# Two transformer blocks in one kernel: the expert gates spread over the partitions by DMA, the first expert behind the router, and a merged norm after the experts

## The chip, the cores and the metric

One Trainium2 chip, one core. The metric is the device time of one execution, in microseconds (us); the median of several executions counts. The engines are called PE (TensorE, matrix products), DVE (VectorE), ACT (ScalarE), POOL (GpSimd) and SP (SyncE). POOL and SP only start transfers here; each has a queue of its own, in which transfers start in the order written.

## The reference

All of it is float32, for 256 tokens of width 1024 and a context of 256 more:

```python
# block 1
h = h + concat(rmsnorm(fox(q_a, k_a, v_a)), rmsnorm(stick(q_b, k_b, v_b))) @ w_out   # from rmsnorm(x) @ w_in
h = h + cross_attention(rmsnorm(h), rmsnorm(mem)) @ w_xo
t = rmsnorm(h)                                  # (256, 1024)
g_val, g_idx = top_k(softmax(t @ w_rg + b_rg), 1)       # 4 groups
e_val, e_idx = top_k((t @ w_re + b_re)[group g_idx], 2) # 4 experts in each
gate = one_hot(experts) * (g_val * softmax(e_val))      # (256, 16)
for e in range(16):                             # hidden width 256
    h = h + gate[:, e:e+1] * ((silu(t @ w_gate[e]) * (t @ w_up[e])) @ w_down[e])
x = rmsnorm(h) * norm_final
# block 2, two layers
for l in range(2):
    sh1, sc1, ga1, sh2, sc2, ga2 = split(silu(c) @ w_mod[l] + b_mod[l])   # the same for ctx
    h = rmsnorm(x) * g1 * (1 + sc1) + sh1       # and hc from the context
    x = x + ga1 * (concat(fourier(h), mlstm(h, hc), mla(h, hc)) @ w_out[l])
    x = x + ga2 * (relu(mod(rmsnorm(x)) @ w_up[l])**2 @ w_down[l])
return rmsnorm(x) * g_final
```

## The kernel before, in words

**Layout.** Activations stand with their features on the 128 partitions: `res` holds 8 feature tiles of 512 columns, 256 of the context (`CTX`) and 256 of the tokens (`LAT`). Weights come from device memory as a stream of 350 pieces of 512 KB, a piece 128 x 1024 float32, into a ring of four (`ring`, SP's queue, L436). Precision is kept by splitting each operand into a high and a low part: ACT rounds a piece (`wh`, L532), DVE subtracts (`wl`, L1568), and PE makes three matmuls for each product, high x high, low x high and high x low (`prod`, L1019, recorded at L995). `split(n)` in the ACT and the DVE program takes the stream's pieces up to n, so its place in the program is the place of the conversion in the engine's order.

**Norms.** ACT squares two feature tiles at a time into slots of `sq` (L558), DVE adds them up in slot 3 (`add_square`, L1586), PE multiplies the sum by a matrix of ones in float32 (`norm`, L1041; the rows read `pair<-sq,table`), ACT makes the root with Ln and Exp (L568, L570), DVE scales (`uv`, L1608), ACT rounds (`uh`), DVE subtracts (`ul`, L1597 or, with a shift, L1599). Around it PE does matmuls whose result nobody reads (`turn_over`, "spins", L1039), in the numbers of the table `SPIN`.

**Modulation vectors.** silu(c) @ w_mod is not done on PE. DVE takes a tile of w_mod (512 KB, POOL's queue, L471) and forms two dot products with it, one for c and one for c_ctx (L1676, L1681). There are 48 such tiles for each layer. They are put by hand between other DVE work: for layer 0, 6 in the stick-breaking part, 4 in the output projection (`out1`), 4 in `xq`, 2 in `xo`, and 32 in the expert loop, two for each expert.

**Router and experts.** `few_rows` makes the 20 logits of each token as rows in a bank of PSUM, ACT copies them (L717), PE turns them to columns (L1276), DVE finds the groups, the experts and the weights in a chain of small operations (L1820 to L1847, results in `small`). Then PE spreads each of the 16 gate columns over all partitions: 64 matmuls of a broadcast column with the identity, ACT copying each pair to `gates` (L727). Eight matmuls with zeros open the four output banks. The experts run in halves of 128 hidden features: `gate_up(i, a, p)` (48 matmuls), then `down` of the half before (24 matmuls). The first expert stands unrolled ahead of the loop, the last behind it. After the last `down` comes norm `fin1`, then norm `n1_0` of the scaled result together with the context, then layer 0's projection.

**Layers.** The first three pieces of a layer's input projection share one loop over the norm's tiles (`together`, L1056). `gate_rows(d)` (DVE) and `log1p_rows` (ACT) prepare the mLSTM gates. After layer 1 comes norm `fin2`, and one transfer stores the result (L442).

Of the kernel before, what the change touches and what calls it, by code (L numbers as in the profile page):

```python
# [22 lines left out]
P = 128  # L23
D = 1024
# [59 lines left out]
NORM_LIST = [("mix", 4, 2), ("mem", 4, 2), ("fox", 2, 2), ("sb", 2, 2), ("xattn", 4, 2), ("ffn", 4, 2), ("fin1", 4, 2)]  # L84
for _l in range(NL):
    NORM_LIST += [(f"n1_{_l}", 8, 1), (f"cq_{_l}", 2, 1) if _l == 0 else (f"cq_{_l}", 1, 2), (f"ckv_{_l}", 1, 1)]
    NORM_LIST += [(f"n2_{_l}", 8, 1)]
# [4 lines left out]
for _i, (_name, _steps, _halves) in enumerate(NORM_LIST):  # L92
# [3 lines left out]
    _add += _steps if _name in LOOPED else _steps - 1  # L96
# [3 lines left out]
for _l in range(NL):  # L100
    U_STEPS += [(f"n1_{_l}", 8), (f"y_{_l}", 10), (f"n2_{_l}", 8)]
# [11 lines left out]
for _name, _n in U_STEPS:  # L113
# [4 lines left out]
SPIN = {"mix": (0, 19, 6), "sb": (5, 5, 6), "xattn": (6, 8, 6), "ffn": (6, 8, 6), "fin1": (24, 0, 4),  # L118
        "n1_0": (34, 17, 5), "n2_0": (7, 17, 5), "n1_1": (18, 17, 6), "n2_1": (5, 8, 5)}
# [3 lines left out]
OUT_NORMS = [_name for _name, _, _ in NORM_LIST if _name not in V_N and _name != "fin1"]  # L123
# [36 lines left out]
MOD_OUT, MOD_XQ, MOD_XO = 4, 4, 2  # L160
MOD_MOE = len(MOD_SB) + MOD_OUT + MOD_XQ + MOD_XO
assert MOD_MOE + N_UNIT == N_MOD
# [58 lines left out]
def build(nc, w_stream, mod_stream, c_rows, ml_dram, table_in, small_in, x_in, mem_in, ctx_in, out):  # L221
    with ExitStack() as stack:
# [92 lines left out]
        hroot = small[:, 140:144]  # L315
        prob = [sq[:, i, :] for i in range(2)]
# [23 lines left out]
        m_ge = tab("m_ge").rearrange("p (k t) -> p k t", k=2)  # L340

# [81 lines left out]
        def _(sp):  # L423
# [17 lines left out]
            sp.wait_ge(S("norm_out"), normed("fin2")[1])  # L441
            sp.dma_start(out, res[:, :, LAT]).then_inc(S("stored"), 16)  # L442
            sp.wait_ge(S("stored"), 16)

        @block.gpsimd
        def _(pool):
# [9 lines left out]

            def mod_loads(l):
# [7 lines left out]
                for g in range(l * N_MOD, (l + 1) * N_MOD):  # L465
                    if g >= l * N_MOD + 2:
                        pool.wait_ge(S("mod_used"), g - 1)
# [55 lines left out]
        def _(act):  # L523
# [36 lines left out]
            def root(name, p, n, width):  # L560
# [3 lines left out]
                if i:  # L564

                    sem, count = normed(NORM_LIST[i - 1][0])
                    act.wait_ge(S(sem), count)
                ch.link(act.activation(rstd[0:p, 0:n], norm_bank(name)[0:p, 0:n], ACT.Ln, bias=tab("eps")[0:p],  # L568
                                       scale=1.0 / width))
# [1862 lines left out]
```

## Time and profile before

| | |
|---|---|
| three runs | 1703.35, 1700.3, 1702.18 us; median 1702.18 |
| the profiled execution | 1705.07 us |
| its span, first to last instruction | 1703.2 us |
| mean granted TensorE clock | 0.98 of full speed |
| PE busy | 1619.8 us (95%) |
| PE weight loads (beside PE) | 1396.6 us (82%) |
| DVE, ACT, POOL busy | 1077.3, 771.8, 96.6 us (63, 45, 6%) |
| read from device memory | 248.84 MB, 147 GB/s over the span |
| chain that ended last, by engine | PE 81%, DVE 12%, ACT 3%, issue 3%, DMA 1% |

Busy times are sums over stages with different limits. The stages, by the profile's time: attention parts up to 252, `out1` to 257, cross-attention with its projections to 336, router 340 to 361, experts 361 to 634, layer 0 from 657, the end at 1703. The profiled execution took 2.9 us more than the median.

### The profile page before, as it was taken

How to read it: one execution, taken by the hardware profiler on the slowest of the kernel's cores; microseconds unless marked ns; L12 is line 12 of the kernel's file. 1: busy time of each engine (PE TensorE's matmuls, PEld its weight loads, DVE VectorE, ACT ScalarE, POOL GpSimd, SP SyncE). 2: the span in 40 equal slices, each digit the busy share in tenths (PEclk: the TensorE clock that was granted, in tenths of full speed). 3: DMA queues.
4: the chain of work that ended last, by engine and by line, in shares of the span. 5: the costliest groups of instructions: out<-in, count | busy, mean ns of one | idle time of the engine just before them, and what ended most of it. 6: DMA issues, size and time to landing. Idle time of an engine off the chain costs nothing.

```text
span 1703.2 us, 27364 instructions
## 1 busy us (share of the span) xinstructions
PE 1619.8 (95%) x9992; PEld 1396.6 (82%) x9992; DVE 1077.3 (63%) x1800; ACT 771.8 (45%) x1306; POOL 96.6 (6%) x160
## 2 busy tenths in 40 slices
PE   7999988999999999999889999999999898899997
PEld 7988567899999996775668788888887785799997
DVE  5544677658888887932584755555556944765554
ACT  5544444444444445343462642134323354665562
POOL 0000100000000000000020000000000000100000
PEclk9999999999999999999999999999999999999998
DMA  7633435337777770332114355455542351155552
GB/s 286 203 121 106 119 121 197 126 106 245 244 246 246 244 236 25 99 123 63 34 29 136 136 189 177 142 165 189 166 145 91 112 158 30 45 166 186 173 184 86
DMA packets 70841, 250.96 MB, mean 147 GB/s; under 512 B 7760, under 2 KB 10976, under 8 KB 70640
## 3 DMA queue, kind: packets, MB, share of 16 engines
q1 hardware_dynamic: 54000, 189.43, 33.9%
q0 software_dynamic: 16768, 60.54, 12.5%
q8 instruction: 49, 0.80, 0.2%
q14 instruction: 24, 0.20, 0.0%
HBM read 248.84 MB, written 1.09 MB: 147 GB/s over the span
## 4 chain that ended last, share of the span: by engine, by line
PE 81%; DVE 12%; ACT 3%; issue 3%; DMA 1%; DVEq 0%; SPq 0%; ACTq 0%
PE pair L995 79%; DVE uv L1608 1%; DVE sq L2086 1%; DVE wl L1568 1%; ACT wh L532 1%; DVE sq L1586 1%; DVE small L1635 1%; DVE sq L1644 1%; PE pair L1162 1%; PE pair L1039 1%; DVE uh_f L1681 1%; ACT sq L558 0%; ACT sq L600 0%; DVE ul L1597 0%; DVE spent L1676 0%
## 5 line engine op out<-in xcount | busy, mean ns | idle before, releaser
L995 PE MATMUL pair<-uh,wh 128*128 128x256 f32 (+3 forms) x1840 | 579.0, 315 | 13.1 <-DVE ul L1597 4.5
L1568 DVE TENSOR_TENSOR wl<-ring,wh 128x1024 fp32r<-128x1024 f32 x350 | 426.9, 1224 | 245.0 <-ACT wh L532 237.9
L995 PE MATMUL pair<-uh,wl 128*128 128x256 f32 (+3 forms) x1840 | 574.3, 312 | 0.0
L995 PE MATMUL pair<-ul,wh 128*128 128x256 f32 (+3 forms) x1840 | 572.7, 311 | 0.0
L532 ACT ACTIVATE wh<-ring 128x1024 fp32r<-128x1024 f32 x350 | 367.5, 1052 | 267.9 <-PE pair L995 262.3
L995 PEld LDWEIGHTS pair<-uh,wh 128*128 128x128 f32 (+1 forms) x1840 | 343.5, 187 | 42.6 <-issue 13.8
L995 PEld LDWEIGHTS pair<-uh,wl 128*128 128x128 f32 (+1 forms) x1840 | 343.6, 187 | 25.6
L995 PEld LDWEIGHTS pair<-ul,wh 128*128 128x128 f32 (+1 forms) x1840 | 343.3, 187 | 24.9
L995 PE MATMUL pair<-hh,wh 128*128 128x512 f32 (+1 forms) x512 | 172.7, 337 | 0.8
L995 PE MATMUL pair<-hh,wl 128*128 128x512 f32 (+1 forms) x512 | 172.0, 336 | 0.0
L995 PE MATMUL pair<-hl,wh 128*128 128x512 f32 (+1 forms) x512 | 172.0, 336 | 0.0
L995 PEld LDWEIGHTS pair<-hh,wh 128*128 128x128 f32 x512 | 97.1, 190 | 12.0 <-issue 2.0
L995 PEld LDWEIGHTS pair<-hl,wh 128*128 128x128 f32 x512 | 97.2, 190 | 10.0
L995 PEld LDWEIGHTS pair<-hh,wl 128*128 128x128 f32 x512 | 97.1, 190 | 10.0
L2207 DVE TENSOR_TENSOR hl<-sq,hh 128x512 f32 (+1 forms) x64 | 35.8, 559 | 95.9 <-ACT hh L954 95.8
L949 ACT ACTIVATE sq<-pair 128x512 f32<-128x512 f32 (+1 forms) x64 | 31.3, 489 | 107.4 <-PE pair L995 107.4
L995 PE MATMUL pair<-hidh,wl 128*128 128x256 f32 x256 | 72.6, 284 | 0.0
L995 PE MATMUL pair<-hidh,wh 128*128 128x256 f32 x256 | 72.5, 283 | 0.0
L995 PE MATMUL pair<-hidl,wh 128*128 128x256 f32 x256 | 72.4, 283 | 0.0
L1039 PE MATMUL pair<-spin 128*128 128x512 f32 x250 | 65.9, 414 | 0.0
L995 PE MATMUL pair<-wh,uh 128*128 128x256 f32 (+1 forms) x192 | 57.2, 298 | 3.0 <-ACT qkp L793 3.0
L471 POOL DMA_DIRECT2D uh_f<-in_mods x48 | 36.0, 751 | 418.1 <-DVE macc L1681 267.4
(259 smaller groups left out, 2080.7 us busy)
## 6 DMA issues: line engine op xcount, KB each, us to landing
ring<-in_w_stream SPq DMA_DIRECT2D x350, 512.0 KB, 3.9
uh_f<-in_mods POOLq DMA_DIRECT2D x48, 512.0 KB, 6.1
mod_w<-in_mods POOLq DMA_DIRECT2D x48, 512.0 KB, 3.8
ml<-ml_dram POOLq DMA_DIRECT2D x4, 512.0 KB, 8.1
table<-in_table SPq DMA_DIRECT2D x1, 1849.5 KB, 12.0
res<-in_x SPq DMA_DIRECT2D x4, 256.0 KB, 3.9
res<-in_mem SPq DMA_DIRECT2D x1, 1024.0 KB, 14.3
res<-in_ctx POOLq DMA_DIRECT2D x1, 1024.0 KB, 6.1
```

The lines of the kernel that those rows point to most:

```text
L471: pool.dma_start(mod_w[l][g % 2], src).then_inc(S(f"mod_in{g % 2}"), 16)
L532: act.activation(wh[:, s, :], ring[:, s, :], ACT.Copy).then_inc(S("w_hi"), 1)
L949: act.activation(r, bank[(b0 + j) % 4][:, 0:n], ACT.Relu).then_inc(S("job_emptied_act"), 1)
L995: ins = pe.matmul(*operands, **flags)
L1039: pe.matmul(bank[b], spin[:, 0:P], spin[:, :], start=True, stop=True)
L1162: last = pe.transpose(bank[6][:, to * P:(to + 1) * P], prob[i % 2][:, j * P:(j + 1) * P], ident)
L1568: tt(wl[:, s, :], ring[:, s, :], wh[:, s, :].bitcast(F32), ALU.subtract).then_inc(S("w_lo"), 1)
L1586: tt(sq[0:p, 3, 0:n], sq[0:p, 3, 0:n], sq[0:p, t % 2, 0:n], ALU.add).then_inc(S("norm_add"), 1)
L1608: last = stt(o, src, g, r, ALU.mult, ALU.mult)
L1635: dve.tensor_reduce(smv(i, 0, 0, g), b, AX_X, ALU.max, negate=True).then_inc(S("sm_max"), 1)
L1644: last = ts(p, p, smv(i, 1, k), None, ALU.mult)
L2207: tt(hl[:, d, 0:n].rearrange("p a b -> p (a b)"), sq[:, 2 + j % 2, 0:n], hh[:, d, 0:n].rearrange("p a b -> p (a b)").bitcast(F32), ALU.sub ...
```

## The change

1. **Norms.** In every norm that isn't in a loop DVE no longer adds the last square. PE sums slot 3, and the slot of the last square with a second pair of ones-matmuls.
2. **Modulation tiles.** In `out1` the fourth tile stands behind the adds and the split instead of ahead of them. The cross-attention takes a tile (at `i == 1`), `xo` three instead of two. The experts have 30 instead of 32, none in the first and none in the last half expert.
3. **Router.** The logits go to a bank of the experts' output (`rt_bank`). PE goes on behind them with the first half expert's gate and up, with the turning of the logits between two of its steps. The context's squares are summed here (norm `ctx`). Of the 20 spins 4 are left.
4. **Gates.** PE turns the 16 gate columns to rows (2 transposes), ACT copies them, and POOL writes them to device memory (`gate_dram`, 16 KB) and reads them back to all partitions in three transfers, of 2, 6 and 8 gates. DVE waits for the first ahead of the first half expert's multiplication, for the other two ahead of the loop.
5. **End of the experts.** `fin1` and `n1_0` become one norm for the tokens: squares are taken with a weight and the epsilon is changed to fit. The context's half of layer 0's first three pieces is done apart, with its own tiles, and around the norm. 75 spins are gone. `fin1`'s own norm and its scaling of `res` go into layer 0's projections.
6. **Layers.** `gate_rows` at j = 11 and 13 instead of 2 and 3; the gate biases and `log1p_rows` move to j = 0 to 3.
7. **Store.** Four transfers of 256 KB, each when its two tiles are scaled, instead of one of 1 MB.

The core of the diff:

```diff
-SPIN = {"mix": (0, 19, 6), "sb": (5, 5, 6), "xattn": (6, 8, 6), "ffn": (6, 8, 6), "fin1": (24, 0, 4),
-        "n1_0": (34, 17, 5), "n2_0": (7, 17, 5), "n1_1": (18, 17, 6), "n2_1": (5, 8, 5)}
+SPIN = {"mix": (0, 19, 6), "sb": (5, 5, 6), "xattn": (6, 8, 6), "ffn": (6, 8, 6),
+        "n2_0": (7, 17, 5), "n1_1": (18, 17, 6), "n2_1": (5, 8, 5)}
...
-MOD_OUT, MOD_XQ, MOD_XO = 4, 4, 2
+MOD_OUT, MOD_XQ, MOD_XAT, MOD_XO = 4, 4, 1, 3
...
-            sp.wait_ge(S("norm_out"), normed("fin2")[1])
-            sp.dma_start(out, res[:, :, LAT]).then_inc(S("stored"), 16)
+            for t in range(4):
+                sp.wait_ge(S("fin2_tile"), 2 * t + 2)
+                sp.dma_start(out[:, 2 * t:2 * t + 2, :], res[:, 2 * t:2 * t + 2, LAT]).then_inc(S("stored"), 16)
...
+            def gate_loads():
+
+                pool.wait_ge(S("gate_rows"), 1)
+                pool.dma_start(gate_dram, logit_rows[0:NE, :]).then_inc(S("gate_out"), 16)
+                pool.wait_ge(S("gate_out"), 16)
+                for k, e in enumerate((slice(0, 2), slice(2, 8), slice(8, NE))):
+                    pool.dma_start(gates[:, e, :], gate_dram[e, :].rearrange("(o e) t -> o e t", o=1)
+                                   .to_broadcast([P, e.stop - e.start, T])).then_inc(S(f"gate_in{k}"), 16)
...
-            for e in range(NE // 2):
-                act.wait_ge(S("gate_full"), e + 1)
-                act.activation(gates[:, 2 * e:2 * e + 2, :], bank[4 + e % 2][:, :].rearrange("p (a t) -> p a t", a=2),
-                               ACT.Copy).then_inc(S("gate_in"), 1)
-            split(S_MOE + 2)
+            root("ctx", P, T, D, rstd[:, T:2 * T])
+            split(S_MOE + 3)
+            act.wait_ge(S("gate_full"), 1)
+            act.activation(logit_rows[0:NE, :], rt_bank[0:NE, 0:T], ACT.Copy).then_inc(S("gate_rows"), 1)
+            split(S_MOE + 4)
...
+                slots = [3] if name in LOOPED or steps == 1 else [3, (steps - 1) % 2]
+                for slot in slots:
+                    if slot != 3:
+
+                        pe.wait_ge(S("norm_sq"), SQ_AT[name] + steps)
+                    for j in range(HALVES[name]):
+                        last = mm(norm_bank(name)[0:p, 0:n], ones[0:p, 0:p], sq[0:p, slot, j * n:(j + 1) * n],
+                                  start=(slot == 3 and j == 0), stop=(slot == slots[-1] and j == HALVES[name] - 1))
...
+            gate_up(0, 0, S_MOE, first=True)
+            norm("ctx", P, T)
+            turn_over(4, 5)
+            pe.wait_ge(S("rt_gate"), 1)
+            for b in range(TB):
+                last = pe.transpose(rt_bank[0:NE, b * P:(b + 1) * P], rt[:, b, 44:60], ident)
+            last.then_inc(S("gate_full"), 1)
...
+            dve.wait_ge(S("gate_in0"), 16)
             moe_unit(0, -1)
+            for k in (1, 2):
+                dve.wait_ge(S(f"gate_in{k}"), 16)
             with dve.Fori(0, MOE_TURNS) as i:
...
+                    for j in range(3):
+                        outs[j] = (outs[j][0](),) + outs[j][1:]
+                        for k in range(3):
+                            half("c1_0", CTX, j, k)
+                    for k in range(3, KT):
+                        if k == 5:
+                            norm("n1_0", P, T)
+                        for j in range(3):
+                            half("c1_0", CTX, j, k)
+                    for k in range(KT):
+                        for j in range(3):
...
+                            last = half("n1_0", LAT, j, k)
```

The order of the instructions, at the two places where most is moved. PE from the router's logits to the expert loop; `L995` and `L1049` are the matmul helper before and after, `rt_gate` is DVE's signal that the weights are ready. Before:

```order
L1276 MATMUL pair<-table,logit_rows 128x20 [waits rt_rows]
L1276 MATMUL pair<-table,logit_rows 128x20
L1039 MATMUL pair<-spin 128x512 x20
L995 MATMUL pair<-table,small 128x128 [waits rt_gate]
L995 MATMUL pair<-table,small 128x128 x7
L995 MATMUL pair<-table,small 128x128 [waits gate_in]
L995 MATMUL pair<-table,small 128x128 x3
```

The last two rows come six times. After, behind the four steps of the first half expert that stand ahead of the logits, the 36 matmuls of its other steps run between the second row and the third:

```order
L1342 MATMUL pair<-table,logit_rows 128x20 [waits rt_rows]
L1342 MATMUL pair<-table,logit_rows 128x20
L1049 MATMUL pair<-sq,table 128x256 [waits norm_add]
L1049 MATMUL pair<-sq,table 128x256
L1049 MATMUL pair<-sq,table 128x256 [waits norm_sq]
L1049 MATMUL pair<-sq,table 128x256
L1093 MATMUL pair<-spin 128x512 x4
L1362 MATMUL pair<-table,small 16x128 [waits rt_gate]
L1362 MATMUL pair<-table,small 16x128
L1049 MATMUL pair<-uh,hidl 128x256 [waits gate_rows,moe_lo]
L1049 MATMUL pair<-uh,hidl 128x256 x7
L1383 UNCONDITIONAL_BRANCH [waits norm_rstd]
```

So the 64 broadcasts with their waits for ACT's copies have left PE. DVE's rows at the start of the experts, after; the branch is the entry of the loop, and behind it stands the subtraction for the sixth piece of the experts' stream:

```order
L1663 TENSOR_TENSOR wl<-ring,wh 128x1024 [waits w_hi] x2
L1972 TENSOR_TENSOR eg<-eg,gates 128x256 [waits moe_silu,gate_in0]
L1978 TENSOR_TENSOR eg<-pair,eg 128x256 [waits moe_eg,moe_up]
L1982 TENSOR_TENSOR hidl<-eg,hidh 128x256 [waits moe_hi]
L2010 UNCONDITIONAL_BRANCH [waits gate_in2,gate_in1]
L2010 ISA
L1663 TENSOR_TENSOR wl<-ring,wh 128x1024 [waits w_hi]
```

Before, the first of these multiplications waited for ACT's eight copies, and nothing stood between the first half expert and the loop. DVE at the end of the experts, from the last piece's subtraction on, before:

```order
L1568 TENSOR_TENSOR wl<-ring,wh 128x1024 [waits w_hi]
L1676 ISA spent,macc<-uh_f_105,uv 128x1024 [waits mod_used,mod_in1]
L1676 ISA macc 128x1
L1681 ISA uh_f_105,macc<-uh_f_105,uv 128x4x256
L1681 ISA macc 128x1
L1893 COPY modv<-macc 128x8 [waits mod_used]
L1914 TENSOR_TENSOR res<-pair,res 128x2x256 [waits moe_down,macc_out]
```

And after:

```order
L1663 TENSOR_TENSOR wl<-ring,wh 128x1024 [waits w_hi] x2
L2025 SCALAR_TENSOR_TENSOR uv<-res,gmod,rstd 128x256 [waits norm_rstd,macc_out]
L2025 SCALAR_TENSOR_TENSOR uv<-res,gmod,rstd 128x256
L1695 SCALAR_TENSOR_TENSOR ul<-uv,modv,uh 128x256 [waits u_h]
L2025 SCALAR_TENSOR_TENSOR uv<-res,gmod,rstd 128x256
L1695 SCALAR_TENSOR_TENSOR ul<-uv,modv,uh 128x256 [waits u_h] x2
L2044 TENSOR_TENSOR res<-pair,res 128x2x256 [waits moe_down] x4
L2025 SCALAR_TENSOR_TENSOR uv<-res,gmod,rstd 128x256 x2
L1695 SCALAR_TENSOR_TENSOR ul<-uv,modv,uh 128x256 [waits u_h] x2
L1682 TENSOR_TENSOR sq<-sq 128x512 [waits norm_sq]
```

The modulation tile has left this place, and the context's first three tiles stand ahead of the residual's adds.

## Rows read from the trace of the kernel before

**Rows 1.** Windows: us, busy of PE, PEld, DVE, ACT, POOL, clock, DMA, GB/s

```profile
346.00:361.00 15.00, 13.54 (x95) 12.18 (x95) 5.14 (x35) 6.19 (x15) 0.00 (x0) 0.99 0.12 36
400.00:600.00 200.00, 200.00 (x1688) 200.00 (x1687) 166.56 (x241) 87.69 (x117) 18.03 (x24) 1.00 0.75 244
634.00:658.00 24.00, 20.17 (x87) 15.52 (x86) 19.07 (x41) 12.23 (x23) 0.00 (x0) 1.00 0.12 38
```

**Rows 2.** The same, spins (L1039) alone: PE, PEld, clock, DMA, GB/s

```profile
634.00:658.00 24.00, 18.18 (x75) 14.02 (x75) 1.00 0.12 38
```

**Rows 3.** PE's waits: us in total, times, longest

```profile
PE pair L995 <- DVE sq L1586: 17.0, 8, 8.1
```

**Rows 4.** Timeline of PE, ones-matmuls: start, us, instruction

```profile
8.12 2.05 PE L995 MATMUL pair<-sq,table 128*128 128x256 f32 x4 [8.12 <-DVE sq L1586]
...
336.42 1.13 PE L995 MATMUL pair<-sq,table 128*128 128x256 f32 x4 [0.80 <-DVE sq L1586]
...
337.20 2.20 PE L1039 MATMUL pair<-spin 128*128 128x512 f32 x8
```

**Rows 5.** The page's costliest groups, DVE's lo parts; timeline of a modulation tile

```profile
L1568 DVE TENSOR_TENSOR wl<-ring,wh 128x1024 fp32r<-128x1024 f32 x350 | 426.9, 1224 | 245.0 <-ACT wh L532 237.9
...
257.94 1.22 DVE L1676 CUSTOM_DVE_ANT_1 spent<-uh_f,uv 128x1024 f32<-128x1024 f32 x1
```

**Rows 6.** Timeline and window at the norm before the cross-attention

```profile
261.77 2.08 PE L995 MATMUL pair<-sq,table 128*128 128x256 f32 x4 [3.07 <-DVE sq L1586]
...
264.84 1.27 DVE L1608 SCALAR_TENSOR_TENSOR uv<-res,table,rstd 128x256 f32<-128x256 f32 x3 [1.99 <-ACT rstd L570]
...
262.00:264.00 2.00, 2.00 (x5) 1.61 (x6) 0.85 (x1) 0.12 (x1) 0.00 (x0) 0.50 0.79 252
```

**Rows 7.** Timeline of DVE and PE around the router

```profile
338.55 1.28 DVE L1608 SCALAR_TENSOR_TENSOR uv<-res,table,rstd 128x256 f32<-128x256 f32 x3 [0.71 <-ACT rstd L570]
...
347.05 0.20 DVE L1820 COPY small<-pair 128x40 f32<-128x40 f32 x1 [0.92 <-PE pair L1276]
...
352.69 7.58 PE L995 MATMUL pair<-table,small 128*128 128x128 f32 x64 [0.91 <-DVE small L1847]
...
375.26 0.28 PE L995 MATMUL pair<-uh,wh 128*128 128x256 f32 x1
```

**Rows 8.** DMA issues: transfer, queue, count, KB each, median us to landing

```profile
ml<-ml_dram POOLq DMA_DIRECT2D x4, 512.0 KB, 8.1
...
ml<-ml_dram POOLq DMA_DIRECT2D x4, 256.0 KB, 7.5
out_dram<-res SPq DMA_DIRECT2D x1, 1024.0 KB, 4.8
...
lw<-ml_dram POOLq DMA_DIRECT2D x2, 256.0 KB, 5.1
...
ml_dram<-rows_buf POOLq DMA_DIRECT2D x4, 8.0 KB, 1.8
```

**Rows 9.** Windows beside ring and modulation loads, and beside broadcasts (columns as rows 1)

```profile
290.00:292.00 2.00, 1.31 (x7) 1.07 (x7) 1.94 (x3) 0.60 (x1) 0.28 (x1) 1.00 1.00 358
...
846.00:848.00 2.00, 1.35 (x11) 0.95 (x9) 0.42 (x2) 0.03 (x1) 0.00 (x0) 1.00 1.00 264
...
850.00:852.00 2.00, 1.44 (x12) 1.25 (x12) 2.00 (x5) 2.00 (x5) 0.00 (x0) 1.00 0.65 145
```

**Rows 10.** Timeline from the last expert to layer 0's first copy

```profile
634.34 5.63 PE L1039 MATMUL pair<-spin 128*128 128x512 f32 x24
...
657.70 0.47 PE L995 MATMUL pair<-uh,wh 128*128 128x512 f32 x1 [0.95 <-DVE ul L1599]
...
674.56 0.58 ACT L793 ACTIVATE qkp<-pair 96x512 f32<-96x512 f32 x1
```

**Rows 11.** Timeline of PE in layer 1's first pieces

```profile
1324.60 0.45 PE L995 MATMUL pair<-uh,wh 128*96 128x512 f32 x1 [1.53 <-DVE wl L1568]
...
1343.32 0.47 PE L995 MATMUL pair<-uh,wh 128*128 128x512 f32 x1 [1.71 <-DVE wl L1568]
```

More of the change, by code:

```diff
@@ L81 @@
 N_LCOLS = 1408
-NORM_LIST = [("mix", 4, 2), ("mem", 4, 2), ("fox", 2, 2), ("sb", 2, 2), ("xattn", 4, 2), ("ffn", 4, 2), ("fin1", 4, 2)]
+NORM_LIST = [("mix", 4, 2), ("mem", 4, 2), ("fox", 2, 2), ("sb", 2, 2), ("xattn", 4, 2), ("ffn", 4, 2), ("ctx", 4, 2),
+             ("n1_0", 4, 2), ("fin1", 4, 2)]
 for _l in range(NL):
-    NORM_LIST += [(f"n1_{_l}", 8, 1), (f"cq_{_l}", 2, 1) if _l == 0 else (f"cq_{_l}", 1, 2), (f"ckv_{_l}", 1, 1)]
+    if _l:
+        NORM_LIST += [(f"n1_{_l}", 8, 1)]
+    NORM_LIST += [(f"cq_{_l}", 2, 1) if _l == 0 else (f"cq_{_l}", 1, 2), (f"ckv_{_l}", 1, 1)]
     NORM_LIST += [(f"n2_{_l}", 8, 1)]
@@ L715, in _ @@
             split(S_RT + AHEAD)
+            act.wait_ge(S("ctx_in"), 16)
+            for t in range(4):
+                square("ctx", t, res[:, 2 * t:2 * t + 2, CTX], P, 512)
             act.wait_ge(S("rt_logits"), 1)
-            act.activation(logit_rows[0:20, :], bank[6][0:20, 0:T], ACT.Identity,
+            act.activation(logit_rows[0:20, :], rt_bank[0:20, 0:T], ACT.Identity,
                            bias=tab("b_route", 20)).then_inc(S("rt_rows"), 1)
@@ L783, in _ @@
                     split(p0 + j + AHEAD)
-                    if j in (1, 2):
-                        log1p_rows(rows[j - 1][:, 1, :], rows[j - 1][:, 2, :], "ml_f", 2 * l + j, "ml_ln")
+                    if l == 0 and j == 1:
+                        for t in range(4):
+                            square("fin1", t, res[:, 2 * t:2 * t + 2, LAT], P, 512)
+                    if l == 0 and j == 5:
+                        root("fin1", P, T, D, sq[:, 2, 0:T])
+                    if j in (2, 3):
+                        log1p_rows(rows[j - 2][:, 1, :], rows[j - 2][:, 2, :], "ml_f", 2 * l + j - 1, "ml_ln")
                     b = full(act, f"mqk_{l}", j)
@@ L1327, in _ @@
             down(MOE_TURNS, UNIT_TURN - 1, S_MOE + N_TURN - 1, final=True)
-            norm("fin1", P, T)
             for l in range(NL):
@@ L1350, in _ @@
                 for j in range(2, 8):
+                    if l == 0 and j == 4:
+                        norm("fin1", P, T)
                     tiles_of(f"mqk_{l}", j, p0 + j, MD if j < 7 else P, cols if j < 4 else ALL)
```

281 lines of the change are left out of this document (177 added, 104 removed).

## The prediction

> **What bounds the kernel now.** I read the page's totals first: TensorE (PE) is busy for 1619.8 of 1703.2 us (in the table above). The windows then say where a change can pay. In the expert loop PE has no gap: 1688 matmuls in 200 us, 0.118 us each, with DVE at 166.56 [rows 1], so there only fewer PE instructions would help. The other two windows of that group lie at its ends. From 346 to 361 PE is busy for 13.54 of 15 us, but with gate broadcasts; from 634 to 658 it is busy for 20.17 of 24, and 18.18 of that is spins [rows 1, 2]. Next I read the waits: PE waits 17.0 us in 8 places for the last add of squares [rows 3]. Last the timelines of each place, for the chain that ends there.
>
> **The added ones-matmuls.** A norm's last pair of ones-matmuls no longer waits for one DVE add, and a second pair is added. An add takes 0.69. A pair takes 0.78 at full clock (336.42 to the spins at 337.20) and about 1.5 at the start of the program, where four rows take 2.05 [rows 4]. So at mix the extra pair costs 1.5 less the add: +0.9. At mem and fox PE runs through and the add was hidden, so the pair is paid whole: +0.85 at mem; at fox, where PE follows a stretch of small matmuls, I take the half clock, twice 0.78 less a little, +1.3. cq_0 gets a second matmul of 512 columns behind small ones too: +1.3 by the same reckoning. fin1's norm, moved into layer 0's projections where PE is full, is two pairs: +1.75. sb 0 and n2_1 -0.5 (a wait for the add). Sum **+5.6**; ends: 0, if the removed adds pay everywhere, and 8, if every pair is paid whole.
>
> **The moved modulation tiles.** One tile is two DVE operations of 1.22 us [rows 5]. At out1 the fourth tile stood ahead of the last adds, and PE stood still for 3.07 until 261.77 [rows 6]. Now the adds go first, but the tile is next and norm xattn's first scaling (264.84) comes behind it: 263.25 earliest, 0.5 gained at the end of it (-0.5), as root and ul follow. In the cross-attention the new tile stands ahead of the third row maximum (L1635); PE's next scores and everything behind it, up to the xo matmuls, move by 2.44 and a little: +2.7. Sum **+2.2**; ends 0 (a gap of the engines there takes it up) and 5.
>
> **The router and the first expert.** Frame: times of the profile, the shift above left out. xo's third tile, 2.44 us, stands between the split and the first scaling at 338.55. Without the last add DVE comes to it 0.9 earlier, so scaling starts at 340.1. The router's matmuls end at 347.5. PE goes on with gate and up of the first half expert, 48 matmuls (5.7), and the logits' transposes inside; DVE starts its chain of small operations at 349.85. That chain took from 347.05 until PE was released at 352.69, 5.6 [rows 7], so weights are ready at 355.45. PE has ended its 48 matmuls at 354.0, does norm ctx (two pairs, 1.6, and a root on ACT that starts behind it), 4 spins, and transposes at 357.0. ACT does root, one split (1.05) and the copy (0.5): gate_rows at 358.4. PE's 8 zeroing matmuls (1.1) and 48 more matmuls end at 365.1. The 64 broadcasts, 7.5 us [rows 7], are gone. What takes their place is a queue of four transfers on POOL. The write of 16 KB: 8 KB took 1.8 [rows 8], so 360.6 with its issue, and the first broadcast moves from 361.9. The first broadcast, 256 KB: 5.1 as lw<-ml_dram, so 365.7, and down(0,0) starts at 367.6 after two multiplications, a rounding and a subtraction (0.4 each), ending at 370.5. The other two are 1.75 MB. This is the **unknown price**. DVE waits for both before the loop, and behind that wait stands the lo split of the sixth piece, which PE's third gate-and-up needs. Rows for broadcasts out of device memory are slow: 512 KB took 8.1 to land [rows 8], and the windows beside them move 264 and 145 GB/s, with ring pieces in it [rows 9]. Rows of the other end: 358 GB/s at 290 to 292, with wholly different rows of memory for each partition. I take 190 GB/s (between 145 and 264, and these are the same kind of transfer): 2.1 MB take 11.0 from 361.9, and two ring pieces between them 2 more: 375. A lo part of 1.22 behind it [rows 5]: PE starts at 376.3 against 375.26 [rows 7], +1.0, and 1.7 more, because after some 5 us with nothing to do the clock falls: behind the gap of 3.07 the window shows 0.50 [rows 6]. **+2.7**; ends -4.7 and +17.4 (rivals A and D).
>
> Here a page stands against my price. The Trainium skill ("DMA: Bandwidth & Descriptors", "Anatomy of one DMA — SWDGE (gpsimd) path") puts such a transfer at about 2.0 us plus bytes over 436 GB/s; the estimate by it for 2 MB is 6.8 us, and my sum would come out near 17 below the profile instead of 10. The trace does not agree for broadcasts of this kernel: 8.1 us for 512 KB.
>
> **The end of the experts.** Before, the last down ends at 634.34 and DVE ends its modulation tile and adds to the residual, PE sums squares, DVE scales, squares again, and layer 0's first matmul starts at 657.70; its three pieces (72 matmuls of 512 columns) end at 674.5, where the first copy starts [rows 10]. After: one norm for both, and the context half of the same matmuls needs nothing of it. DVE makes context tiles from 634.1 (the modulation tile that ran until 636.4 is gone), adds at 636.9 to 639.3, and PE does 36 of the context half's matmuls meanwhile. The last squares are in at 643.5, the two pairs end at 645.4, root at 646.75, and with a scaling, a rounding and an ul the LAT half starts at 648.6: 72 matmuls of 256 columns, 8.5 us, end at 657.0. With the short pauses between context tiles I put 2.3 on it for a lower clock: 659.3. **-15.1**; ends -18 (no clock loss) and -9 (rival C). The total of PE work left is 2 x 8.5 + 1.9 = 18.9 us behind 634.4, so nothing below 653.3 is possible.
>
> **Layers and tail.** gate_rows at j = 11 and 13 leaves the place where, in layer 1, PE waits 1.53 and 1.71 for a lo split [rows 11]: **-3.2** (ends -3.2 and 0, if the convolutions or the later place wait for the same). In layer 0 the same rows plus fin1's eight scalings stand at j = 10 to 13; DVE has spare time there, nothing. The store of 1 MB landed in 4.8 [rows 8]; now four of 256 KB, three of them under the scaling. The last: between 1.8 (8 KB) and 4.8, by bytes 2.6, and 2.9 behind its three neighbours: **-1.9**.
>
> **Sum.** 5.6 + 2.2 + 2.7 - 15.1 - 3.2 - 1.9 = -9.7 against 1705.07, the profiled execution's time, so 1695.4. The median of the three runs lies 2.9 below that execution: **1692.5 us**.
>
> **Rivals.** A, the loads are fast (0.2): at 358 GB/s all three land at 367.7, down(0,0) ends at 370.6 and the third gate-and-up follows at once: -4.7 in place of +2.7, no clock loss, sum -17.1, median **1685.1**. For it: every other load of this size; against it: the broadcast rows. B, they are slower than I take (0.12): four broadcasts of 256 KB, issued within 1.5 us, land 7.5 after issue each [rows 8], 1.05 MB in 9 us or 118 GB/s; the third gate-and-up is 6.7 later, sum -3.0, **1699.2**. C, the clock (0.12): 75 spins are taken out between 634 and 658 and the matmuls that replace them come with pauses for context tiles. Behind the 3.07 us gap of [rows 6], the window has PE at 0.50 though spins ran on. Should the half clock hold for the stage, 72 matmuls of 256 columns take twice 8.5, of which some 6 stay on the path: sum -3.7, **1698.5**. The Trainium skill ("TensorE: Matmul & The Clock Gate", Part 1) has the throttled state as the default that activity releases, which speaks against taking spins out; the trace agrees in that gap. D, slower (0.06): the loads stand behind mod loads and ring pieces, with all partitions reading one 16 KB, at about 80 GB/s. gate_in2 lands at 390, the third gate-and-up waits until 391, PE idle for 20 us: 15.7 and the clock's 1.7, +17.4 in place of +2.7, sum +5.0, **1707.2**. It decides from a landing after 385 on (the sum is zero there). That the change does not do what it says I can leave out: the order of the engines shows every move.
>
> **How the numbers follow.** The forecast has 0.5, A 0.2, B 0.12, C 0.12, D 0.06. A difference of 0.2% (3.4 us) is about what a measurement of this kernel can tell from none. Of B and C, at -3.0 and -3.7, half lies within it; so same 0.12, slower 0.06, faster 0.82. The range is 1685 to 1700: it takes in A's value, B and C, and the bounds of the small terms (+2.4 and -5.6 at the ones-matmuls, 3.2 at the layers); outside lie D, the sum of several bad ends and A with a good clock.
>
> **What would show it.** In the changed kernel's profile: gates<-gate_dram in the list of DMA issues with its time to landing (mine: some 5, 9 and 13 us); PE's wait for wl ahead of the third gate-and-up, 5.8 us; the LAT half's first matmul some 14 us behind the last down, with the clock of the window of 24 us behind it at 0.8 or more; no wait for wl in layer 1's first pieces; PE waits for adds of squares down from 17.0. It would be wrong if the loads land within 7 us of their issue or beyond 25, or if the clock in that window is 0.5.

## The result, and the profile after

| | before | after |
|---|---|---|
| median | 1702.1 us (4 runs) | 1676.88 us (4 runs, 1672.28 to 1681.26) |
| ratio | | 0.9861, 95% interval 0.9836 to 0.9885 |
| span of the profiled execution | 1703.2 us | 1673.3 us |
| mean granted TensorE clock in it | 0.980 | 0.984 |

Two later series of the same changed kernel gave ratios of 0.9888 (0.9858 to 0.9918) and 0.9877 (0.9857 to 0.9898). All 17 of its runs together have the median 1679.3; 49 runs of the kernel before in three later series have 1699.7, and they reach from 1691.6 to 1706.7. So the change is worth about 20 us, not the 30 that the two first profiles differ by, and not the 9.7 that I forecast. The predicted range ended at 1685 and the median lies below it.

Each execution also has its mean granted clock on record, and that explains most of the spread. Over the 49 runs of the kernel before it goes from 0.978 (1706.7 us) to 0.989 (1693.4); a straight line through them gives 1.39 us for each 0.001, and leaves a scatter of 1.6 us of 3.5. Measured from that line, that is against the kernel before at the same granted clock, the changed kernel is 22.2, 22.6 and 23.3 us faster in its three series. The line is an estimate from these runs, used again below.

The page after, its totals and the part of its waits that answers to [rows 3] (before, PE waited 17.0 us in 8 places for the last add):

```profile
PE 1596.2 (95%) x9959; PEld 1383.8 (83%) x9959; DVE 1069.2 (64%) x1790; ACT 768.2 (46%) x1308; POOL 98.6 (6%) x164
```

```profile
PE pair L1049 <- DVE sq L1682: 7.9, 2, 7.7
```

The waits for adds are gone but for the program's start (7.7). Part of them only moved: PE now waits 8.2 us in 5 places for the low parts of L1693, where it waited 4.5 in 4 for those of L1597. A wait of 4.5 us is new: the first `down` waits for the first gates (PE's first row below). The router in the timelines of POOL, DVE and PE, which answers to [rows 7]:

```profile
351.59 0.53 POOL L469 DMA_DIRECT2D gate_dram<-logit_rows  x1 [16.96 <-ACT logit_rows L755]
353.56 1.63 POOL L472 DMA_DIRECT2D gates<-gate_dram  x3 [1.45 <-DMA gate_dram<-logit_rows]
```

```profile
360.79 0.43 DVE L1972 TENSOR_TENSOR eg<-eg,gates 128x256 f32<-128x256 f32 x1 [7.29 <-DMA gates<-gate_dram]
...
365.86 1.23 DVE L1663 TENSOR_TENSOR wl<-ring,wh 128x1024 fp32r<-128x1024 f32 x1 [3.21 <-DMA gates<-gate_dram]
```

```profile
362.78 0.58 PE L1049 MATMUL pair<-hidh,wh 128*128 128x256 f32 x1 [4.50 <-DVE hidl L1982]
...
368.06 0.29 PE L1049 MATMUL pair<-uh,wh 128*128 128x256 f32 x1
```

The three broadcasts land 7.2, 9.0 and 10.9 us after their own issues, where I had some 5, 9 and 13. The last is issued at 354.7 and lands at 365.6, 12.0 us after the first issue; my sum had 14.4 (375 less 360.6). The loads didn't creep. Windows of 2 us over them (the columns are those of rows 1) show 323 and 415 GB/s, with PE all but idle:

```profile
354.00:356.00 2.00, 2.00 (x20) 2.00 (x19) 0.00 (x0) 0.00 (x0) 1.19 (x3) 1.00 0.82 287
356.00:358.00 2.00, 2.00 (x20) 2.00 (x18) 0.00 (x0) 0.00 (x0) 0.00 (x0) 1.00 0.64 188
358.00:360.00 2.00, 0.28 (x3) 0.07 (x1) 0.00 (x0) 0.00 (x0) 0.00 (x0) 1.00 0.99 323
360.00:362.00 2.00, 0.00 (x0) 0.00 (x0) 0.85 (x2) 0.22 (x1) 0.00 (x0) 0.81 0.99 415
362.00:364.00 2.00, 1.22 (x5) 1.23 (x6) 0.42 (x1) 2.00 (x4) 0.00 (x0) 0.50 0.70 295
```

The last two windows also show the half clock (0.50, that is 1.2 of 2.4 GHz) behind the wait of 4.5 us; `down` ran at it. The end of the experts, PE and then ACT, which answers to [rows 10]:

```profile
628.57 0.36 PE L1049 MATMUL pair<-uh,wh 128*128 128x256 f32 x1 [1.27 <-DVE ul L1695]
...
636.37 0.92 PE L1049 MATMUL pair<-sq,table 128*128 128x256 f32 x3
```

```profile
650.25 0.58 ACT L847 ACTIVATE qkp<-pair 96x512 f32<-96x512 f32 x1
```

From the last `down`'s end (627.30) to layer 0's first copy it is 22.95 us where it was 40.06. The merged norm's ones-matmuls run 9 us behind the last `down`, with the context's matmuls on both sides of them. The tokens' half starts at 641.28, 14.0 behind the last `down` as forecast, and the window of 24 us behind it has a granted clock of 0.93.

Because single executions wander, I read the stages from all profiles of this study: four of the kernel before and its variants, ten of the changed kernel and its variants, each only where the stage is untouched. The figures are lengths between the same two PE instructions, in us; the difference is that of the means.

| stage | before | after | difference | forecast |
|---|---|---|---|---|
| first norm to norm mem | 32.0, 32.3, 33.8 | 35.5 in seven of ten; 33.7, 35.2, 36.5 | +2.7 | +0.9 (mix; the pair alone 1.5) |
| norm mem to the forgetting attention's scores | 58.9, 61.3, 61.3 | 59.2 in eight of ten; 61.1, 63.1 | -0.8 | +0.85 (mem) |
| the attention parts, to the spins of norm sb | 123.6, 124.8 | 117.7 to 123.5, eight profiles | -3.8 | +1.3 (fox) |
| end of out1 to xq | 8.5, 9.5, 9.9 | 7.7 | -1.6 | -0.5 |
| xq to the scores | 23.5 to 23.7 | 25.0 to 25.1 in six of seven; 23.5 | +1.2 | 0 |
| scores to xo | 20.2 to 21.1 | 21.1 to 23.2 | +1.6 | +2.7 |
| end of xo to the third gate-and-up | 40.2 to 41.2 | 38.7 to 40.5, four profiles | -1.2 | +2.7 |
| last down to layer 0's first copy | 40.1 to 40.2 | 22.9 to 23.0 | -17.1 | -15.1 |
| from there to layer 1's norm | 624.8 to 626.6 | 624.2 to 630.0 | +2.1 | +3.05 |
| that norm to n2_1 | 202.4, 202.8 | 197.0 to 198.5 | -5.0 | -3.7 |
| n2_1 to fin2 | 190.9 | 188.4 to 191.4 | -1.0 | 0 |
| fin2 to the end | 10.1 | 7.9 to 8.0 | -2.2 | -1.9 |

The first row starts behind the wait for the add, so it holds the price of the extra pair alone. In the first profiles that is 1.7 (3.19 us for the ones-matmuls instead of 1.49), near the 1.5 of the forecast; what the removed add gives back lies ahead of the row.

### The profile page after: what moved, and what is told of

Its sections match the earlier page's. It is cut to its first block, busy times and chain, and to the rows that moved or that the text cites. A ratio compares the mean times of both kernels' runs of the same rounds, so it can differ in the third digit from the quotient of the medians.

```text
span 1673.3 us, 27283 instructions
## 1 busy us (share of the span) xinstructions
PE 1596.2 (95%) x9959; PEld 1383.8 (83%) x9959; DVE 1069.2 (64%) x1790; ACT 768.2 (46%) x1308; POOL 98.6 (6%) x164
## 4 chain that ended last, share of the span: by engine, by line
PE 83%; DVE 9%; ACT 3%; issue 3%; DMA 1%; DVEq 0%; SPq 0%; ACTq 0%
PE pair L1049 81%; ACT wh L552 1%; DVE uv L1704 1%; DVE sq L2228 1%; PE pair L1223 1%; DVE sq L1740 1%; DVE wl L1663 1%; DVE small L1731 1%; PE pair L1093 1%; DVE ul L1693 0%; DMA gates<-gate_dram 0%; DMA uh_f<-in_mods 0%; DVE uh_f L1777 0%; ACT sq L621 0%; DVE spent L1772 0%
## 5 line engine op out<-in xcount | busy, mean ns | idle before, releaser
L1049 PE MATMUL pair<-uh,wh 128*128 128x256 f32 (+3 forms) x1864 | 583.5, 313 | 14.0 <-DVE ul L1693 8.2
L1049 PE MATMUL pair<-uh,wl 128*128 128x256 f32 (+3 forms) x1864 | 577.9, 310 | 0.0
L1049 PE MATMUL pair<-ul,wh 128*128 128x256 f32 (+3 forms) x1864 | 576.4, 309 | 0.0
L1049 PEld LDWEIGHTS pair<-uh,wh 128*128 128x128 f32 (+1 forms) x1864 | 347.9, 187 | 42.1 <-issue 14.3
L1049 PEld LDWEIGHTS pair<-uh,wl 128*128 128x128 f32 (+1 forms) x1864 | 347.8, 187 | 24.0
L1049 PEld LDWEIGHTS pair<-ul,wh 128*128 128x128 f32 (+1 forms) x1864 | 347.5, 186 | 23.4
L1049 PE MATMUL pair<-hh,wh 128*128 128x512 f32 (+1 forms) x512 | 172.7, 337 | 0.8
L1049 PE MATMUL pair<-hh,wl 128*128 128x512 f32 (+1 forms) x512 | 172.0, 336 | 0.0
L1049 PE MATMUL pair<-hl,wh 128*128 128x512 f32 (+1 forms) x512 | 172.0, 336 | 0.0
L1049 PEld LDWEIGHTS pair<-hh,wh 128*128 128x128 f32 x512 | 97.1, 190 | 11.9 <-issue 2.0
L1049 PEld LDWEIGHTS pair<-hh,wl 128*128 128x128 f32 x512 | 97.1, 190 | 10.1
L1049 PEld LDWEIGHTS pair<-hl,wh 128*128 128x128 f32 x512 | 97.2, 190 | 10.0
L1049 PE MATMUL pair<-hidh,wh 128*128 128x256 f32 x256 | 73.7, 288 | 4.5 <-DVE hidl L1982 4.5
L1049 PE MATMUL pair<-hidh,wl 128*128 128x256 f32 x256 | 73.6, 288 | 0.0
L1049 PE MATMUL pair<-hidl,wh 128*128 128x256 f32 x256 | 73.5, 287 | 0.0
L1049 PE MATMUL pair<-wh,uh 128*128 128x256 f32 (+1 forms) x192 | 57.2, 298 | 3.0 <-ACT qkp L847 3.0
L1777 DVE CUSTOM_DVE_ANT_0 mod_w<-mod_w,mod_c 128x1024 f32<-128x1024 f32 x48 | 58.5, 1219 | 0.0
L1777 DVE CUSTOM_DVE_ANT_1 uh_f<-uh_f,uv 128x1024 f32<-128x1024 f32 x48 | 58.5, 1218 | 0.0
```

Source lines behind the costliest of these rows:

```text
L1049: ins = pe.matmul(*operands, **flags)
L1777: return dve.tensor_tensor_reduce(out=mod_w[l][k], in0=mod_w[l][k], in1=mod_c[l][which], scale=1.0, scalar=0.0, op0=ALU.mult, op1=ALU.add, ...
```

## The experiments

**The changed kernel again, twice.** No edit.

> The changed kernel once more, unchanged, as the base of the three below on the same chip. Theory 'structure': the stretches in which TensorE is granted half its clock follow from PE's own gaps, so they fall at the same places as in the first profile (258 to 262, 288 to 292, 336 to 341, 360 to 368, 630 to 634, 756 to 766, 798 to 804, 1374 to 1380) and none at 92 to 100; time 1674 to 1680. Rival 'luck': they move from execution to execution, and one of about 3 us at 92 to 100, as the kernel before had, may come back; time 1672 to 1684.

> The changed kernel, unchanged, as the base of a_sb_fill on the same chip, and for a third profile: 1676 to 1681. The part behind the experts (last down to the first copy of layer 0) should take 22.9 to 23.0 us again; the loop of layer 1's MLP takes 2.72 or 2.83 for a tile (both were seen with this kernel).

Medians 1681.07 (6 runs) and 1679.31 (7), spans 1679.3 and 1670.2. The third profile has most of its half-clock stretches where the first had them, but not those at 630 to 634 (0.61 in the first) and 798 to 804 (0.51 in the first, 0.93 in the third). The second lacks the one behind the last `down` too. It has one that the first lacks, behind PE's wait of 2.13 us for the last stick-breaking head, a wait that stands in all three:

```profile
214.00:228.00 14.00, 11.74 (x24) 6.17 (x25) 3.44 (x7) 2.41 (x4) 0.00 (x0) 0.55 0.10 35
```

The first profile has 1.00 in the same window. The attention part takes 122.35 in the second profile against 118.06 and 118.08 in the others. Both theories hold in part: places belong to the program, but not each comes in each execution. The experts' end took 22.93 and 22.98, as expected.

**Fox's add put back in the changed kernel.**

```diff
-    _add += _steps if _name in LOOPED else max(_steps - 2, 0)
+    _add += _steps if _name in LOOPED else _steps - 1 if _name in ADDED else max(_steps - 2, 0)   # ADDED = ("fox",)
```

> The changed kernel with one thing undone: norm fox gets its DVE add of the last square back, and one pair of ones-matmuls. Theory 'blocked queue': before, that add stood in DVE's order ahead of a modulation tile and of the stick-breaking operations and waited there for ACT's squares; PE's wait of 1.92 us at that place and the half clock behind it came from it. Then this run is 4 to 7 us slower than the changed kernel, with a PE wait for sbt of about 2 us behind the norm. Rival 'price of a pair', by which I forecast +1.3 for the removal: this run is 1 to 1.5 us faster than the changed kernel.

Median 1680.19 (5 runs) against 1681.07: no difference that these runs can tell. PE's wait came back as expected, and the half clock behind it (194 to 201):

```profile
194.21 1.19 PE L1050 MATMUL pair<-qk 64*128 64x256 f32 x2 [1.92 <-DVE sbt L1837]
```

The changed kernel waits 0.51 here (the row at 192.41 of its first profile). But this execution lacked the stretch at 214 to 228, and its attention part took 121.8. So the 4 to 7 us slower that I expected didn't come; whether it is the rival's 1 to 1.5 us faster, five and six runs can't tell.

**Fox alone, in the kernel before.**

```diff
+                if name == "fox":
+                    return
```
(in DVE's `add_square`; PE waits for the square and sums slots 3 and 1)

> The kernel before with norm fox alone changed: no DVE add of its last square, a second pair of ones-matmuls. Forecast's term: +1.3 (about 1702 against 1700.7). Theory 'blocked queue': PE's wait of 1.92 for sbt doesn't come, and the part from the first stick-breaking scores to its end takes 118 to 123 us instead of 123.6 to 124.8; runs 2 to 4 below before.

Ratio 0.9998 (0.9983 to 1.0013), 12 runs. PE's wait is 0.51 and not 1.92, so the queue was blocked as the theory says, but the gain of 2 to 4 us isn't there. Its profile had half-clock stretches at 94 to 100 and 216 to 226, and took 121.7 for the part. The add's removal is worth less than 3 us, and it isn't a loss of more than 2.2; my +1.3 lies inside these bounds.

**All norms, in the kernel before.** The diff of the change for `add_square`, `norm` and the count of the adds, nothing else. It also gives an extra pair to `fin1` and `n1_0`, which are still two norms in this kernel.

> The kernel before with the norms' part of the change alone (no last add, a second pair of ones-matmuls, in every norm that isn't in a loop). The forecast's own term was +5.6 less the +1.75 of the moved norm, so about 1706 (+3.5). Theory 'blocked queue': the fox part turns by some -6 to -7, out1's add saves about 1 more, so 1696 to 1700 (-2 to -6).

Ratio 0.9991 (0.9969 to 1.0013): -1.6 us, between -5.3 and +2.2. My +3.9 for this part (5.6 less 1.75; the +3.5 above is a slip) is outside, and so is the far end of the rival's range. The trace has what the extra pairs cost and save: +1.7 at mix (35.5 us to norm mem), and 8.6 us from out1's end to xq, against 8.5, 9.5 and 9.9. The granted clocks say more. Their mean is 0.987 over these 12 runs, where the kernel before has 0.984, and against the line of the kernel before at the same clock they are 3.6 us slower (+-0.8 by their own scatter). By this estimate the pairs cost about what I forecast, and the full clock, which was granted for longer, gave it back. Which of the removed waits raised the clock wasn't tried; at fox alone (the run above) it stayed at 0.984.

**Gates by matmuls in the changed kernel.**

```diff
-            for b in range(TB):
-                last = pe.transpose(rt_bank[0:NE, b * P:(b + 1) * P], rt[:, b, 44:60], ident)
+            for e in range(NE // 2):     # 4 broadcast matmuls each, into two banks
+                last = mm(gate_banks[e % 2][...], small[:, w:w + 1].to_broadcast([P, P]), ident, start=True, stop=True)
...
-                    if g == MOD_MOE + 2:
-                        gate_loads()
```

> The changed kernel, but the gates are spread by 64 matmuls and 8 copies on ACT, behind the first half expert's gate and up, instead of by the DMA. No transfer, no wait of 4.5 us for the first gates, no half clock behind it. Theory 'the DMA is a loss here': PE pays 7.5 us and the first down follows at once, so the third gate-and-up comes 1 to 3 us earlier than with the DMA: 1 to 3 us faster than the changed kernel. Rival 'the DMA pays': the matmuls cost their 7.5 us and the waits that they replace were 1.2 and 4.5 with 2 of half clock, so the same within 0.5, or slower by up to 3 if ACT's copies hold the broadcasts back.

Median 1677.64 (4 runs) against 1681.07 (6), within their noise. From the logits' transposes to the third gate-and-up 24.27 us, against 25.30, 24.57 and 23.42 in the three profiles with the DMA. So the way of the gates makes no difference that can be seen: the 7.5 us of matmuls and the transfers' latency cost the same. `down` ran at half clock, wholly or in part, in all eight profiles with the DMA, and at full clock in the two with matmuls, which had no wait there. That the stage is shorter than before must then come from what both kernels have, the first gate-and-up in the time of DVE's chain; that was not undone by itself.

**The broadcasts twice.**

```diff
+                pool.wait_ge(S("gate_in1"), 16)
+                pool.wait_ge(S("gate_in2"), 16)
+                for k, e in ((1, slice(2, 8)), (2, slice(8, NE))):   # the same two transfers again
```

> The changed kernel, but the second and third broadcast are made twice, the second time when both have landed, and DVE waits for the second time: 1.75 MB more on the disputed path. Theory 'the broadcast moves like any other load' (320 to 415 GB/s in the first profile): the third gate-and-up comes some 6 to 8 us later, latency of the second pair with it. Rival 'slow broadcasts', my 190 GB/s: 10 to 12 us later. The rate can be read from windows of 2 us without the other engines' noise.

POOL issues the second pair at 372.54 and DVE goes on at 379.90, 7.4 us for 1.84 MB with the latency. The windows:

```profile
374.00:376.00 2.00, 0.06 (x1) 0.00 (x0) 0.00 (x0) 0.00 (x0) 0.00 (x0) 1.00 0.93 310
376.00:378.00 2.00, 0.00 (x0) 0.00 (x0) 0.00 (x0) 0.00 (x0) 0.00 (x0) 0.56 1.00 411
378.00:380.00 2.00, 0.00 (x0) 0.00 (x0) 0.10 (x1) 0.00 (x0) 0.00 (x0) 0.50 0.38 160
```

The logits-to-third-gate-and-up stretch is 31.15 us against 23.4 to 25.3: 6 to 8 more, as the theory of an ordinary load said. A broadcast out of device memory, with rows of 6 and 8 KB for a partition, moves 411 GB/s. My 190 is refuted as the rate at which these transfers move. By the rule of the Trainium skill ("DMA: Bandwidth & Descriptors", "Anatomy of one DMA — SWDGE (gpsimd) path"), 1.84 MB would take an estimated 6.2 us; the trace's 7.4, for two transfers and POOL's issue, is 1.2 above it.

**The broadcasts in a chain of 1, 7 and 8 gates.**

```diff
-                for k, e in enumerate((slice(0, 2), slice(2, 8), slice(8, NE))):
+                for k, e in enumerate((slice(0, 1), slice(1, 8), slice(8, NE))):
+                    if k == 1:
+                        pool.wait_ge(S("gate_in0"), 16)
```

> The changed kernel with the three broadcasts cut as 1, 7 and 8 gates, and the second and third issued only when the first has landed. Theory 'shared queue': the first broadcast of 256 KB took 7.2 us from issue because the other two ran beside it; alone, 128 KB land in 3 to 4.5, so the wait of 4.5 us ahead of the first down shrinks to 1 to 2, and the other two, at the 320 to 415 GB/s of the first profile, land at most 1 us later than they did (12.3 us behind the first issue). Rival 'latency': a broadcast out of device memory takes 6 to 7 us whatever its size; then the first wait stays at 4 and the others land 6 us later, 5 us slower.

One execution, 1679.12 us. 128 KB landed in 4.6 us where 256 KB took 7.2, and the first wait shrank from 4.50 to 1.94. The wait for the others grew:

```profile
361.40 0.38 PE L1051 MATMUL pair<-hidh,wh 128*128 128x256 f32 x1 [1.94 <-DVE hidl L1984]
...
368.23 0.38 PE L1051 MATMUL pair<-uh,wh 128*128 128x256 f32 x1 [2.20 <-DVE wl L1665]
```

Logits to third gate-and-up 24.45 us, no gain: what had been one wait is two. The experts behind it took 260.9 us where the changed kernel takes 259.2, a loss of 1.6. The rival, 6 to 7 us whatever the size, is refuted. The theory of the shared queue fits the first landing, though the run changed size and company together: at 411 GB/s half the size is an estimated 0.3 us of the 2.6. It gives nothing, since the loop waits for all gates.

**Spins in three waits.**

```diff
-SPIN = {"mix": (0, 19, 6), "sb": (5, 5, 6), "xattn": (6, 8, 6), "ffn": (6, 8, 6),
+SPIN = {"mix": (0, 19, 6), "sb": (5, 5, 6), "xattn": (6, 16, 6), "ffn": (6, 16, 6),
...
                     pe.wait_ge(S("w_lo"), p0 + 2)
+                    turn_over(6, 7)
```

> The changed kernel with spins in three waits of PE: 8 more behind the norms xattn and ffn (waits of 2.36 and 2.35), 6 behind the last down (wait of 1.27). Theory 'gap, then half clock': the half-clock stretches at 258 to 262, 336 to 341 and 630 to 634 go, each worth 1 to 1.5 us; the trace gains 3 to 4 by layer 0 and the runs' median about 3. Rival 'the clock falls for another reason' (a fixed spacing in time, or the float32 matmuls): the stretches stay or move, no gain, and the spins themselves cost up to 1.

The three stretches are gone; the first two:

```profile
258.00:262.00 4.00, 4.00 (x19) 3.33 (x18) 3.83 (x6) 1.04 (x3) 0.02 (x1) 1.00 0.43 128
336.00:341.00 5.00, 4.30 (x21) 2.97 (x19) 5.00 (x15) 2.26 (x6) 0.75 (x1) 1.00 0.60 202
```

In the changed kernel's first profile these windows have 0.60 and 0.66, and 630 to 634 has 0.61:

```profile
258.00:262.00 4.00, 4.00 (x25) 4.00 (x24) 3.58 (x11) 2.65 (x6) 0.00 (x0) 0.60 0.31 114
```

(This execution ran 4 to 6 us behind, and none of its windows at 262 to 290, 341 to 362 and 634 to 700 has the half clock either.) For two of the three places all profiles together bear the gap theory out. Behind the waits of 2.3 us at xattn and ffn the half clock came in six of seven profiles each, and with the spins in none of three each. For the third place this run shows nothing: behind the last `down` four of the seven profiles without spins have full clock too. The theory is wrong about the price in two of three. xq to the scores went from 25.0 to 23.2 (and took 23.5 in the one profile that had the wait and kept full clock). But the rows of the router took 7.52 as before, and the experts' end 22.94 as before, since DVE's tiles set the pace there: in all ten profiles it takes 22.93 to 22.98, in three at half clock and in seven at full. Median 1676.24 (5 runs), ratio 0.9874 (0.9852 to 0.9896): no gain that the runs can tell.

**The same, and spins for the last stick-breaking head.**

```diff
+                    if h == NF:
+                        turn_over(8, JOBS.number("xkv", 6) % 4)
```

> a_fill3 with 8 spins more, in PE's wait of 2.13 us for the last stick-breaking head. Theory 'gap, then half clock': no half-clock stretch at 214 to 228, the part from the first stick-breaking scores to its end takes 118 us and not 121 to 124, runs 2 to 3 us below a_fill3 (1676). Rival 'luck': the stretch comes back at another place of the small matmuls (it did at 184 to 190 and at 94 to 100 with no such gap ahead), and nothing is gained on the median.

No half clock at 214 to 228 and 119.0 us for the attention part, as the gap theory said. But that is one profile, and four of the nine changed kernels without these spins have full clock there as well, so it proves little. Median 1678.05 (6 runs) against 1679.31 of the changed kernel on the same chip: unclear. The mean granted clock did rise, from 0.983 to 0.988, without a gain of that size in the time.

**Spins and matmul gates.** The edits of both.

> The fills of a_fill3 together with the gates spread by matmuls. If the DMA is a loss of about 1 us and the half-clock stretches go, 4 to 5 us below the changed kernel; if neither holds, the same.

Median 1678.26 (5 runs), ratio 0.9882 (0.9861 to 0.9903). Its profile has the shortest span of all, 1669.8, and that means little: the same kernel ran from 1671.6 to 1680.6. No version here beats the change measurably.

**gate_rows and the store, in the kernel before.** The two pieces of the diff alone.

> The kernel before with two parts of the change alone: gate_rows at j = 11 and 13, and the store in four transfers. Forecast terms -3.2 and -1.9, about 1696 to 1697. The trace should show no wait for wl at layer 1's first pieces (1.53 and 1.71 before), and some 3 us instead of 5 from the last scaling to the end. Rival: the rows' new place makes PE wait there, then 0 of the 3.2. As this kernel is the same as before up to layer 0, its half-clock stretches up to 700 us also tell whether those of before (94 to 100, 196 to 202, 220 to 226) belong to the program: theory 'gap' has the last two come back, and the first, which had a gap of 0.7 ahead of it, not surely.

Ratio 0.999 (0.9974 to 1.0005): -1.7 us, and -5.1, the sum of my two terms, is outside. The trace differs from the median again. The end took 8.00 instead of 10.11, as forecast. Of layer 1's two waits one is left:

```profile
1318.82 0.45 PE L996 MATMUL pair<-uh,wh 128*96 128x512 f32 x1 [1.53 <-DVE wl L1569]
```

In the changed kernel neither is there. I had put both to `gate_rows`. Ahead of the first stand DVE's four additions of the gate biases (1313.61 to 1316.65), which this kernel left in place and the change moved; that the first wait goes with them is read from the order, not tried. The stretch from layer 1's norm to n2_1 took 199.2 (202.4 and 202.8 with nothing changed, 197.0 to 198.5 with all). At the same granted clock these ten runs are 4.0 us faster (+-0.9) by the line of the kernel before, nearer to my 5.1.

## Why the prediction was wrong, by its steps

The direction was right, and so was the order of the terms: the experts' end is by far the largest, layers and store next. The size was not: -9.7 forecast, about -20 over all runs. No single term makes up the 10 us between them. The steps, with the table above:

- **The router** (+2.7; measured about -1.2). This is the step that failed, the largest miss that the traces pin to one place. It rested on 190 GB/s, read from the time to landing of `ml<-ml_dram` and from the windows beside it [rows 8, 9]. The time to landing holds queueing behind its neighbours. The windows of 264 and 145 GB/s have the DMA engines busy for 1.00 and 0.65 of the time, so that broadcast is dearer per byte than the gates', which moved 411 GB/s at 1.00; why wasn't tried. They were the nearest rows by name and not by kind. The doubled load took 7.4 us for 1.84 MB. That the last landing was off by only 2.4 us (14.4 forecast, 12.0 measured, from the first issue) is luck: the rate was too low by half, and against it I had too little for the latency and for the ring pieces that moved first (188 to 287 GB/s in the first two windows). Of rival A, its cause was right and its price not: the loads were fast once they moved, but its 5.8 us to the last landing were 12.0. The rest of the miss: I charged 1.7 for a half clock of which 1.0 showed (DVE's low part ended at 367.09, PE went on at 368.06), and some 0.5 us came from ahead of the transfers.
- **The experts' end** (-15.1; -17.1 in every profile). The mechanism was right to the step. The 2.3 for a lower clock was a charge on a stage in which DVE sets the pace: with the half clock (0.61 at 630 to 634 in the first profile) and without it the stage takes 22.9 to 23.0 us. Rival C fails the same way.
- **Layer 1** (-3.7 with n2_1's; -5.0). The two waits were right. The rows' move alone gave 3.4 us with one of the two waits gone (1.71), so about 1.7 came on top with it; what else stood behind the rows I didn't look for. Another 1.0 behind n2_1 was in no term of the forecast (the last section).
- **The ones-matmuls** (+5.6 in all; the part tested alone, +3.9 forecast, -1.6 measured with 2.2 as its upper end). The rows show the price of a pair right: 1.7 at mix against 1.5, and an estimated 3.6 for the part tested alone at the same granted clock. The step left out that the granted clock could rise with them. It also left out what an add costs that waits in DVE's order: at fox a modulation tile and the stick-breaking operations stood behind it, and PE's wait of 1.92 came from there. That wait is shown, by taking it out and by putting it back; a gain in the median from it isn't. In the rows-and-store kernel, which keeps the add, the wait is missing too: there PE ran at half clock just ahead of it (0.51 at 180 to 186) and came later. The attention parts' -3.8 goes with the half-clock stretches there. The one behind the wait of 2.13 us came in nine of the thirteen profiles without spins, in all four of the kernel before and in five of nine of the changed one. Whether the change or chance made it rarer is open.
- **Modulation tiles.** Right in sign; out1 -1.6 against -0.5, and +1.6 against +2.7 in the cross-attention. What I missed is 1.5 us in xq: a wait of 2.3 us moved behind norm xattn, and the clock fell behind it in six of seven profiles (25.0 to 25.1 us); in the seventh it did not, and the stage took 23.5 as before.
- **The store** (-1.9; -2.2). Right: the four transfers of 256 KB landed in 2.4 to 2.6.
- **The range.** It took the rivals one at a time and left out that several terms could be at their good end together: with the ends that stand in the text (router -4.7, experts' end -18, ones-matmuls 0, tiles 0) the sum is -27.8, or 1674. Terms whose errors don't depend on each other should widen a range, and I had six of them.

What stays open: the rows of the table add up to some -25, the medians say -20 and the runs at the same granted clock -22 to -23; and 4 to 17 runs with a scatter of 3 to 5 us can't settle 2 us. The merged norm was not run alone either: its -17.1 rests on the stage, which takes 40.1 to 40.2 in the four profiles without it and 22.9 to 23.0 in the ten with it. Nor were the moved tiles.

## What to carry to other kernels

Read a transfer's price from windows in which nothing else limits it, or issue the transfer a second time and take the difference; the time to landing of a queued transfer is no bandwidth. Before charging a lower clock or an added matmul, ask which engine sets the pace of that stage. When many independent terms are estimated, let the range hold several of them at their good end, and compare stages over several profiles before a difference of two single ones is believed. Set the time of each run beside its mean granted clock: two kernels then differ by less scatter, and a gain by the clock is told from one by the work.

## What the runs showed of the hardware that I had not expected

Half clock comes behind waits of PE of some 2 us, but not always: behind the same wait of 2.13 us it fell in the second profile (0.55 over 14 us) and not in the first and third, and in nine of the thirteen profiles that have this wait. It also came with no wait over 0.7 us, in stretches of small matmuls: at 94 to 100 in two of four profiles of the kernel before and its variants. The rows-and-store kernel is the same program up to there and had full clock:

```profile
94.00:100.00 6.00, 6.00 (x27) 5.76 (x27) 2.70 (x5) 1.97 (x5) 0.00 (x0) 0.50 0.10 40
```

Such stretches cost some 3 to 4 us apiece (the attention part took 118.1 without one and 122.35 with one), and the mean granted clock, in which they show, goes with most of the spread of the runs (correlation -0.89 over 49 runs of the kernel before).

A broadcast read out of a buffer of 16 KB moved 407 to 415 GB/s in windows of 2 us, more than the 358 of an ordinary load in [rows 9].

Last, a loop of layer 1's MLP, its last 16 tiles, ran at two speeds in the same changed kernel, 2.72 us for a tile in the first and third profile and 2.83 in the second, with the same instructions and at full clock. ACT's first operation of a tile waits longer; first profile, then second:

```profile
1605.85 0.39 ACT L1003 ACTIVATE sq<-pair 128x256 f32<-128x256 f32 x1 [0.63 <-PE pair L1049]
```

```profile
1611.47 0.39 ACT L1003 ACTIVATE sq<-pair 128x256 f32<-128x256 f32 x1 [0.73 <-PE pair L1049]
```

That is 1.7 us between two executions of one program. All four profiles of the kernel before and its variants had 2.83, and seven of the ten of the changed kernel and its variants 2.72, so the change may have a part in it. Its cause was not looked for.
